# Start of a transformer block on one core: x sent transposed as well, one DMA queue in order of need, other orders on ScalarE and VectorE

## What is computed

```python
mem_n = rmsnorm(mem, g_mem)
h = rmsnorm(x, g_mix_pre)
proj = h @ w_in                              # 1024 x 2048: v, u, q, k
q, k, v, u = split(proj)                     # q, k, v: 4 heads; u: 512 wide
q = apply_partial_rope(q, cos, sin)          # cos, sin of positions * inv_freq
k = apply_partial_rope(k, cos, sin)
da = diff_attention(q, k, v, lam)            # lam from exp of two dots of 64
# pooling: mean over a window of 2, 4, 8 or 16 tokens back, minus u
pooled = causal_multiscale_pool(u)
po = einsum('bsgc,gcd->bsgd', pooled, w_pool) * pool_scale
mix = concat([da, po]) @ w_out
x = x + rmsnorm(mix, g_mix_post)
kv = mem_n @ w_xkv                           # for cross attention, later
```

## Time and profile before

| | us |
|---|---|
| median of 3 runs (1018.59 to 1018.97) | 1018.89 |
| the profiled execution | 1019.62 |
| its span | 1017.5 |
| PE busy in the span | 1006.7 |
| VectorE, ScalarE busy | 761.8, 539.4 |
| GpSimd busy | 31.9 |

### The profile page before, as it was taken

One profiled execution on the slowest core, in us unless ns is written; L12 is line 12 of the kernel. 1 busy time (PEld: TensorE's weight loads), 2 busy tenths in 40 slices (PEclk: granted clock), 3 DMA queues, 4 the chain that ended last, 5 costly groups with the idle time before them and its releaser, 6 DMA issues.

```text
span 1017.5 us, 17213 instructions
## 1 busy us (share of the span) xinstructions
PE 1006.7 (99%) x6902; PEld 903.4 (89%) x6902; DVE 761.8 (75%) x1041; ACT 539.4 (53%) x757; POOL 31.9 (3%) x50
## 2 busy tenths in 40 slices
PE   8999999999999999999999999999999999999997
PEld 7999899898888889998888888889999988888885
DVE  6898687698886457897788888437788869888632
ACT  6886484565454347875464544337533365454431
POOL 1000100000000001000000000001000100000000
...
GB/s 338 396 138 164 164 228 124 84 231 222 187 206 186 188 164 273 195 138 124 125 166 211 202 188 187 202 194 199 168 126 167 83 131 246 202 202 181 195 83 42
DMA packets 27437, 184.46 MB, mean 181 GB/s; under 512 B 3216, under 2 KB 3488, under 8 KB 6128
## 3 DMA queue, kind: packets, MB, share of 16 engines
...
q10 hardware_dynamic: 432, 0.37, 0.1%
HBM read 182.53 MB, written 1.05 MB: 180 GB/s over the span
## 4 chain that ended last, share of the span: by engine, by line
PE 99%; ACT 1%; DVE 0%; issue 0%; ACTq 0%
PE GT L1939 11%; PE D L1939 11%; PE GT L1902 10%; PE GT L1904 9%; PE GT L1903 9%; PE D L1902 8%; PE D L1904 8%; PE D L1903 8%; PE GT L1945 6%; PE D L1945 5%; PE D L2669 1%; PE GT L2106 1%; PE GT L2164 1%; PE D L2527 1%; PE GT L2542 1%; PE GT L2125 1%
## 5 line engine op out<-in xcount | busy, mean ns | idle before, releaser
L1043 DVE TENSOR_TENSOR s_wlo<-s_raw,s_whi 128x2048 fp32r<-128x2048 f32 (+1 forms) x164 | 355.4, 2169 | 97.0 <-ACT s_whi L518 95.4
L518 ACT ACTIVATE s_whi<-s_raw 128x2048 fp32r<-128x2048 f32 (+1 forms) x164 | 297.9, 1820 | 140.7 <-PE D L1904 86.1
L1939 PE MATMUL GT<-s_x,s_whi 128*128 128x512 f32 x512 | 124.5, 390 | 0.0
L1939 PE MATMUL D<-s_x,s_whi 128*128 128x512 f32 x480 | 116.4, 390 | 0.0
L1939 PEld LDWEIGHTS GT<-s_x,s_whi 128*128 128x128 f32 x512 | 93.6, 188 | 17.3
L1902 PE MATMUL D<-s_whi,s_hTh 128*128 128x512 f32 x264 | 103.0, 390 | 0.0
L1904 PE MATMUL D<-s_whi,s_hTl 128*128 128x512 f32 x264 | 102.7, 389 | 0.0
L1903 PE MATMUL D<-s_wlo,s_hTh 128*128 128x512 f32 x264 | 102.7, 389 | 0.0
L1939 PEld LDWEIGHTS D<-s_x,s_whi 128*128 128x128 f32 x480 | 87.8, 188 | 16.3
L1902 PE MATMUL GT<-s_x,s_whi 128*128 128x256 f32 x336 | 94.5, 281 | 0.0
L1904 PE MATMUL GT<-s_x,s_wlo 128*128 128x256 f32 x336 | 93.3, 278 | 0.0
(11 more groups left out here) (410 smaller groups left out, 1786.5 us busy)
## 6 DMA issues: line engine op xcount, KB each, us to landing
s_raw<-in_stream SPq DMA_DIRECT2D x164, 1024.0 KB, 4.8
...
```

Source lines behind the costliest of these rows:

```text
L518: nc.scalar.activation(high(u, n), raw[:, u % RING, 0:n], ACT.Copy)\
L1043: nc.vector.tensor_tensor(low(u, n), raw[:, u % RING, 0:n], high(u, n), ALU.subtract)\
L1939: return nc.tensor.matmul(o[:, f, :], high_block(u, kt, f), x2[:, kt, :], start=start, stop=stop)
```

## The change

A second copy of x, transposed on the host (`xT`), is loaded in quarters into `xraw`, which lies in y's memory, alternating with unit 0's quarters; ScalarE and VectorE split it straight from there, and PE's 16 transposes go. x itself comes behind unit 3; its squares move behind the first splits. The constants come in one transfer, and mem, memT and the pool matrices move from GpSimd's queue to SyncE's, between units 4 and 8. Unit 1 comes in halves. `zeros()`, a product of zeros, stands ahead of the second and fourth step of `first_unit` and behind it. Units 1 to 3 all run as `early_unit`, with banks G0, G1, D0, D1 by `first_bank`; the counters of reads stay those of G0 and G1. Splits 6 and 7 move behind the tables and the first rotation copy, mem's squares ahead of split 5, `mem_rstd` ahead of unit 5, lambda's work behind split 10. The angles are one chain of fewer steps, with the cosine from the sine's reduced angle. Pooling's product of the first tile on the second has 16 columns for 128. A GpSimd load of a row of gains waits for unit 7.

```diff
...
 x2 = sb(ctx, "x2", [P, KT, 2 * S], F32R)
+xraw = y[:].rearrange("p t n -> p (t n)").rearrange("p (k n) -> p k n", k=KT)
 xTh, xTl = x2[:, :, 0:S], x2[:, :, S:2 * S]
...
     return (u - base) % 2
+def first_bank(u):
+    return (G[0], G[1], DB[0], DB[1])[u]
 def pow_at(name):
...
 def _(sp):
+    for i in range(4):
+        sp.dma_start(xraw[:, 2 * i:2 * i + 2, :], xT_in[:, 2 * i:2 * i + 2, :])\
+            .then_inc(sem(f"piece_in{i}"), 16)
+        sp.dma_start(raw[:, 0, 512 * i:512 * i + 512], stream[0, :, 512 * i:512 * i + 512])\
+            .then_inc(sem(f"piece_in{i + 1}"), 16)
+    sp.dma_start(raw[:, 1, 0:UNIT // 2], stream[1, :, 0:UNIT // 2]).then_inc(sem("second_in"), 16)
+    sp.dma_start(raw[:, 1, UNIT // 2:UNIT], stream[1, :, UNIT // 2:UNIT]).then_inc(landed[1], 16)
+    sp.dma_start(raw[:, 2, :], stream[2, :, :]).then_inc(landed[2], 16)
+    sp.dma_start(cst[:], consts_in).then_inc(sem("cst_in"), 16)
+    sp.dma_start(raw[:, 3, :], stream[3, :, :]).then_inc(landed[3], 16)
     for t in range(NT):
-        sp.dma_start(xn[:, t, :], x_in[t * P:(t + 1) * P, :]).then_inc(sem(f"x_in{t}"), 16)
-    for i in range(4):
-        sp.dma_start(raw[:, 0, 512 * i:512 * i + 512], stream[0, :, 512 * i:512 * i + 512])\
-            .then_inc(sem(f"first_in{i}"), 16)
-    for j in range(1, RING):
-        sp.dma_start(raw[:, j, :], stream[j, :, :]).then_inc(landed[j], 16)
-        if j == 1:
-            sp.dma_start(cst[:, CONST_FIRST:], consts_in[:, CONST_FIRST:]).then_inc(sem("cst_in"), 16)
-    with sp.Fori(1, N_UNITS // RING) as i:
+        sp.dma_start(xn[:, t, :], x_in[t * P:(t + 1) * P, :]).then_inc(sem("x_in"), 16)
+    def early(u):
+        sp.wait_ge(lo_ready, u - RING + 1)
+        sp.dma_start(raw[:, u % RING, :], stream[u, :, :]).then_inc(landed[u % RING], 16)
+    early(4)
+    sp.dma_start(vx[:], mem_in.rearrange("(t p) d -> p t d", p=P)).then_inc(sem("mem_in"), 16)
+    early(5)
+    sp.dma_start(memT[:], memT_in).then_inc(sem("memT_in"), 16)
+    early(6)
+    early(7)
+    sp.dma_start(poolm[:], poolm_in).then_inc(sem("pool_in"), 16)
+    sp.dma_start(wpool, wpool_in).then_inc(sem("pool_in"), 16)
+    with sp.Fori(2, N_UNITS // RING) as i:
...
         pool.dma_start(gb[:], rows_in[r, :].partition_broadcast(P)).then_inc(sem("gb_in"), 16)
+    pool.wait_ge(hi_ready, 2)
+    pool.dma_start(posi[:], pos_in.partition_broadcast(P)).then_inc(sem("pos_lam_in"), 16)
+    pool.wait_ge(sem("cst_in"), 16)
     power("x0.0")
     power("x0.1")
-    pool.wait_ge(hi_ready, 2)
-    pool.dma_start(posi[:], pos_in.partition_broadcast(P)).then_inc(sem("pos_in"), 16)
-    pool.dma_start(lam[:], gains_in[:, LAM:]).then_inc(sem("lam_in"), 16)
-    pool.wait_ge(sem("norm_sq"), 4)
-    pool.wait_ge(hi_ready, 5)
-    pool.dma_start(vx[:], mem_in.rearrange("(t p) d -> p t d", p=P)).then_inc(sem("mem_in"), 16)
-    pool.dma_start(memT[:], memT_in).then_inc(sem("memT_in"), 16)
-    pool.dma_start(poolm[:], poolm_in).then_inc(sem("pool_in"), 16)
-    pool.dma_start(wpool, wpool_in).then_inc(sem("pool_in"), 16)
-    pool.dma_start(gb[:], rows_in[0, :].partition_broadcast(P)).then_inc(sem("gb_in"), 16)
     power("mem.0")
     power("mem.1")
+    pool.wait_ge(hi_ready, 7)
+    pool.dma_start(lam[:], gains_in[:, LAM:]).then_inc(sem("pos_lam_in"), 16)
+    pool.wait_ge(unit_done, 8)
+    pool.dma_start(gb[:], rows_in[0, :].partition_broadcast(P)).then_inc(sem("gb_in"), 16)
     power("subln")
...
-    act.dma_start(cst[:, 0:CONST_FIRST], consts_in[:, 0:CONST_FIRST]).then_inc(sem("cst_first_in"), 16)
     act.dma_start(gains[:], gains_in[:, 0:LAM]).then_inc(sem("gains_in"), 16)
-    norm_squares(0, xn, lambda c: chunk(y, c), parts=range(2))
+    act.wait_ge(sem("warm_in"), 1)
+    nc.scalar.activation(small[:, 0:1], gb[:, 0:1], ACT.Copy)
+    x_scratch = kxT[:].rearrange("p (c k) n -> p c (k n)", c=4)
     act.wait_ge(sem("gains_in"), 16)
     for i in range(4):
-        norm_hi(0, xTh, (2 * i, 2 * i + 1))
-        act.wait_ge(sem(f"first_in{i}"), 16)
+        if i == 0:
+            act.wait_ge(sem("piece_in0"), 16)
+        for kt in (2 * i, 2 * i + 1):
+            nc.scalar.activation(xTh[:, kt, :], xraw[:, kt, :], ACT.Copy, scale=gain("g_mix_pre", kt))\
+                .then_inc(sem("norm_hi"), 1)
+        act.wait_ge(sem(f"piece_in{i + 1}"), 32 if i < 3 else 16)
         nc.scalar.activation(whi[:, 0, 512 * i:512 * i + 512], raw[:, 0, 512 * i:512 * i + 512],
                              ACT.Copy).then_inc(sem("first_hi") if i < 3 else hi_ready, 1)
-    for j in range(1, 4):
-        split(j)
+    act.wait_ge(sem("second_in"), 16)
+    nc.scalar.activation(whi[:, 1, 0:UNIT // 2], raw[:, 1, 0:UNIT // 2], ACT.Copy).then_inc(sem("first_hi"), 1)
+    act.wait_ge(landed[1], 16)
+    nc.scalar.activation(whi[:, 1, UNIT // 2:UNIT], raw[:, 1, UNIT // 2:UNIT], ACT.Copy).then_inc(hi_ready, 1)
+    split(2)
+    split(3)
+    norm_squares(0, xn, lambda c: x_scratch[:, c, :], parts=range(2))
     u0 = BASE["in"]
...
         for t in range(NT):
-            ins = nc.scalar.activation(dst[:, t, :], halves(G[bank(u)][:])[:, t, :], ACT.Copy,
+            ins = nc.scalar.activation(dst[:, t, :], halves(first_bank(u)[:])[:, t, :], ACT.Copy,
                                        scale=rstd[:, POW_COL[f"x0.{t}"]])
         ins.then_inc(bank_read[bank(u)], 1)
+    split(u0 + RING)
     evac_scaled(u0, vn[:, :, 0:256])
-    split(u0 + RING)
     evac_scaled(u0 + 1, vn[:, :, 256:512])
+    act.wait_ge(sem("mem_in"), 16)
+    norm_squares(1, vx, lambda c: x_scratch[:, c, :])
     split(u0 + 1 + RING)
...
         evac_scaled(u0 + 2 + j, un[:, :, 256 * j:256 * j + 256])
-        split(u0 + 2 + j + RING)
-    act.wait_ge(sem("angles"), 2)
+    act.wait_ge(sem("angles"), 1)
     nc.scalar.activation(sinT[:], sinT[:], ACT.Sin).then_inc(sem("trig"), 1)
-    nc.scalar.activation(cosT[:], cosT[:], ACT.Sin).then_inc(sem("trig"), 1)
-    act.wait_ge(sem("mem_in"), 16)
-    mem_scratch = kxT[:].rearrange("p (c k) n -> p c (k n)", c=4)
-    norm_squares(1, vx, lambda c: mem_scratch[:, c, :])
+    nc.scalar.activation(cosT[:], cosT[:], ACT.Sin, scale=-1.0).then_inc(sem("trig"), 1)
+    split(u0 + 2 + RING)
     rope_raw(0, u0 + 4, qraw, "_a")
+    split(u0 + 3 + RING)
+    rope_raw(1, u0 + 5, qraw, "_a")
+    mem_hi()
     split(u0 + 4 + RING)
-    rope_raw(1, u0 + 5, qraw, "_a")
+    rope_raw(2, u0 + 6, qraw, "_a")
     split(u0 + 5 + RING)
-    mem_hi()
-    rope_raw(2, u0 + 6, qraw, "_a")
-    split(u0 + 6 + RING)
     for gp in range(2):
...
         nc.scalar.activation(sm[:, gp, :, :], halves(TB[gp][:]), ACT.Copy).then_inc(sem("pooled_out"), 1)
+    split(u0 + 6 + RING)
     rope_raw(3, u0 + 7, qraw, "_a")
...
     nc.vector.memset(gb[:, 0:512], 0.0).then_inc(sem("warm_in"), 1)
-    dve.wait_ge(sem("x_in1"), 16)
-    for c in range(2, 4):
-        nc.vector.tensor_tensor_reduce(chunk(y, c), chunk(xn, c), chunk(xn, c), 1.0 / D, 0.0,
-                                       ALU.mult, ALU.add, ss[:, 16 + c:17 + c])\
-            .then_inc(sem("norm_sq"), 1)
-    norm_mean(0, "x0", 0)
-    norm_mean(0, "x0", 1)
     dve.wait_ge(sem("gains_in"), 16)
     for i in range(4):
-        norm_lo(0, xTh, xTl, (2 * i, 2 * i + 1))
+        dve.wait_ge(sem("norm_hi"), 2 * i + 2)
+        for kt in (2 * i, 2 * i + 1):
+            nc.vector.scalar_tensor_tensor(xTl[:, kt, :], xraw[:, kt, :], gain("g_mix_pre", kt),
+                                           xTh[:, kt, :], ALU.mult, ALU.subtract)\
+                .then_inc(sem("xT_ready"), 1)
         if i < 3:
...
     split(2)
+    x_scratch = kxT[:].rearrange("p (c k) n -> p c (k n)", c=4)
+    dve.wait_ge(sem("x_in"), 32)
+    for c in range(2, 4):
+        nc.vector.tensor_tensor_reduce(x_scratch[:, c, :], chunk(xn, c), chunk(xn, c), 1.0 / D, 0.0,
+                                       ALU.mult, ALU.add, ss[:, 16 + c:17 + c])\
+            .then_inc(sem("norm_sq"), 1)
+    norm_mean(0, "x0", 0)
+    norm_mean(0, "x0", 1)
     split(3)
     split(4)
-    dve.wait_ge(sem("pos_in"), 16)
+    dve.wait_ge(sem("pos_lam_in"), 16)
     dve.wait_ge(sem("cst_in"), 16)
...
     link(nc.vector.tensor_scalar(ang, ang, const("invfreq"), None, ALU.mult))
-    def angle(out_, shift, turn):
-        link(nc.vector.tensor_scalar(turns, ang, 1.0 / two_pi, turn, ALU.mult, ALU.add))
-        link(nc.vector.tensor_scalar(turns, turns, magic, None, ALU.add))
-        link(nc.vector.tensor_scalar(turns, turns, -magic, None, ALU.add))
-        link(nc.vector.scalar_tensor_tensor(out_[:], turns, -c1, ang, ALU.mult, ALU.add))
-        link(nc.vector.scalar_tensor_tensor(out_[:], turns, -c2, out_[:], ALU.mult, ALU.add))
-        link(nc.vector.scalar_tensor_tensor(out_[:], turns, -c3, out_[:], ALU.mult, ALU.add))
-        link(nc.vector.tensor_scalar(out_[:], out_[:], shift, 3.1415925, ALU.add, ALU.min))
-        nc.vector.tensor_scalar(out_[:], out_[:], -3.1415925, None, ALU.max).then_inc(sem("angles"), 1)
-    angle(sinT, 0.0, 0.0)
```

(90 more changed lines are left out.)

43 lines of the change are left out of this document (17 added, 26 removed).

## The result

The changed kernel takes 1021.44 us (median of 14 runs, 1020.5 to 1022.3 but for one disturbed run) against 1019.16 for the kernel before (median of 14). The ratio is 1.0020, with an interval of 1.0012 to 1.0027: slower by 2.3 us, where 0.7 less was forecast. Repeated later, it was 1021.23 against 1019.4 (1.0017, 1.0008 to 1.0026).

What follows compares the result with a forecast made beforehand. PE's stream was taken as the bound: 1.7 us gained at unit 1, 1.5 at unit 4, 1.1 at unit 5's end, 0.9 at the transposes, less 0.2 for semaphore delays: 0.7, so 1018.89 becomes 1018.2; range 1016.7 to 1020.2.

Steps and rivals of the forecast that it cites:

- Head start at unit 1: Start of PE's stream: x^T in interleaved quarters, no transposes; unit 1 starts at 14.4 for 16.11, 1.7 us earlier.
- Units 1 to 3: PE from unit 1 through the spread of rstd: at the old pace, ends at 31.4 to 31.7.
- unit 4 at 31.6: Unit 4 waits for the read of unit 2 out of G0, free at 31.5; starts 1.5 us earlier than 33.10.
- the row behind the landing: ScalarE's work from the landing of unit 4's weights (22.9) to the read of unit 2: 8.6 us.
- near 23: x lands behind unit 3 at about 20.0; squares, means and powers end near 23, wanted at 31: hidden by 8 us.
- rival 4: Transfers bound unit 4: with quarters 1.0 apart its weights land at 25.0, unit 4 0.5 late, 1020.0 us; chance 0.12.
- Units 4 to 7: Unit 4 to the first transposes: ScalarE and VectorE cause waits of 0.35 and 0.2; 0.9 us earlier remains.
- the row from unit 5's end: ScalarE without idle time from unit 5's end: 14.7 us until the last rotation copy starts at 58.1.
- Narrower band: Pooling: 8 instructions of 128 moving columns become 16; no gain, or 0.9 us if they were free.
- From the heads on one constant shift: Attention heads to the end: later phases keep the shift, as VectorE's copies wait for PE in each head.
- The pace: Long later stretches: PE's spacing changing between 114 and 118 ns per 256-column matmul could add or take 1 us.
- Batching rule: Skill's 1 MiB transfer advice, set aside for the rows: unit 4's weights would land at 26 to 27, 1021 to 1022 us.

Runs made afterwards that it cites:

- e7: The kernel before, run once more with nothing edited: 1018.78 us, one run.
- e6: The changed kernel, run once more with nothing edited: 1021.23 us, ratio 1.0017 to the kernel before.
- e1: The changed kernel, but before unit 4 PE waits for only one read out of bank G0 (unit 0's): 1019.76 us, ratio 1.0007.
- e5: The changed kernel with e1's wait, split 10 behind the pool mix, no zeros, VectorE's splits 11 to 18 one place later: 1019.30 us, ratio 1.0000.
- the second pair: The profiles of e7 and e6, the kernel before and the changed kernel run again unedited: spans 1016.7 and 1019.0 us.

## Why the prediction was wrong

Point by point, by its own steps; the first profile of after unless said otherwise.

- **Head start at unit 1**: 14.4 forecast, 14.87 measured. The pieces were slower: they came at 0.84 apart, not 0.65, and the last weights quarter at 10.25, not 9.5. Each `zeros()` was estimated at 0.5 and cost 0.43: from 14.51 to 15.18 for two steps that take 0.24 without it. But the reference point was poor: in e7 the kernel before has unit 1 at 15.14, not 16.11, as its transposes found the clock up. With 15.26 in e6, the head start was between nothing and 1.2 us, for 1.7 forecast. The 9.60 of unit 0 I took as the kernel's, and it was this execution's.
- **Units 1 to 3**: 31.4 to 31.7 with the spread forecast, 32.4 measured: 0.5 come from unit 1 and 0.2 from the restart behind the zeros, and all three ran at 118 ns, which was the upper end of the estimate.
- **The step that failed: unit 4 at 31.6.** The mechanism was named (bank G0, the read of unit 2, margin nil), and the row behind the landing was sized right, 8.6 for 8.5. The landing was not: 24.14 for 22.9, of which 0.75 come with the pieces and 0.4 with x and the positions (3.3 us for 1.1 MB). And rstd was put "near 23", hidden by 8 us; it came at 26.5 and ScalarE, not PE, wanted it first, 0.4 before it was there. Of these 3.5 us, 1.6 are x, which landed at 21.64 for 20.0, and 1.9 its squares, means and powers, which took 4.9 us for 3; GpSimd's two powers alone are 3.08. The landing and the wait for rstd together make 1.6: 33.19. They are not two separate losses: in this profile rstd came last, so an earlier landing of unit 4's weights alone would have gained nothing. The whole is the mechanism of rival 4, whose own landing (25.0, and unit 4 at 33.6) was 0.9 too late.
- **Units 4 to 7**: the row from unit 5's end was forecast at 14.7 to the last rotation copy and measured at 14.83 (45.22 to 60.05), and the cosine product came at 62.96 for 61.1, the scores at 66.69 for 64.8, the probabilities at 74.26 for 72.4: each 1.9 late. Of this 1.6 come from unit 4; most of the rest lies between unit 5's last products and ScalarE's first read of them, at 45.22, for which the sum had 0.1. e1 to e5 showed both rows as bounds, one behind the other.
- **Narrower band**: nothing, as forecast. Pooling took 2.60 us (50.67 to 53.27), as before (50.32 to 52.91).
- **From the heads on one constant shift**: right up to 697 us, within 0.2.
- **The pace** stood last in the prediction as what "could add or take 1 us", and had no chance of its own. It took 0.2 in each of units 6 and 7 and 0.8 behind 698 us in the first profile. It should have been in the range.
- **Batching rule**: the landing it gave, 26 to 27, was further off than that from the rows.

The median is 2.3 higher. The start loses 0.9 in the first pair of profiles and 2.4 in the second (unit 10 at 74.5 and 75.1, for 73.6 and 72.6 before), 1.7 on average. The rest is pace and clock in parts of unknown size: the second pair has the same pace behind 698 us, and its spans differ by 2.3.
